# Strassen's scheme in the up projection of a gated MLP, with the down projection as a second stage, on one Trainium2 core

## The reference, cut to what matters

```python
D_MODEL, D_FF, DEPTH, CONV_W = 1024, 2816, 2, 3
def conv_gated_mlp(h, w_up, conv_w, conv_b, w_down):
    u = h @ w_up                              # (tokens, 2 * 2816)
    up = jnp.pad(u, ((0, 0), (1, 1), (0, 0)))
    c = conv_b
    for i in range(CONV_W):                   # width 3 along the tokens, each channel by itself
        c = c + up[:, i:i + s] * conv_w[i]
    gate, val = jnp.split(c, 2, axis=-1)
    return (jax.nn.gelu(gate, approximate=True) * val) @ w_down
...
x = x + rms_norm(conv_gated_mlp(rms_norm(x, norm_ffn_pre[l]), ...), norm_ffn_post[l])
```

## Time and profile before

| | |
|---|---|
| median of 3 runs | 3652.87 us (3652.32 to 3656.74) |
| the profiled execution | 3653.27 us |
| its span in the profile | 3651.5 us |
| PE busy | 3561.5 us (98%), 17785 matmuls |
| DVE, ACT, POOL busy | 50%, 42%, 32% |
| mean traffic of the DMA engines | 64 GB/s |
| MLP of the first layer | about 917 to 1870 us |
| MLP of the second layer | about 2721 us to the end |

### The profile page before, as it was taken

One profiled execution on the slowest core, in us unless ns is written; L12 is line 12 of the kernel. 1 busy time (PEld: TensorE's weight loads), 2 busy tenths in 40 slices (PEclk: granted clock), 3 DMA queues, 4 the chain that ended last, 5 costly groups with the idle time before them and its releaser, 6 DMA issues. The chain is left out here.

```text
span 3651.5 us, 49117 instructions
## 1 busy us (share of the span) xinstructions
PE 3561.5 (98%) x17785; PEld 2948.8 (81%) x17785; DVE 1837.5 (50%) x3004; ACT 1523.0 (42%) x2535; POOL 1153.3 (32%) x841
## 2 busy tenths in 40 slices
PE   8999999999999999999999999999999999999998
PEld 7788777778888888888767887777778888888886
DVE  4134879946333334343551358799353333433335
ACT  4344878955221222211342368788442122211213
POOL 1143554434322212211342435544342212211213
PEclk9999999999999999999999999999999999999999
DMA  5442221023111111111324423111221111111113
GB/s 176 124 114 69 77 69 34 23 81 104 47 35 40 38 37 34 40 40 34 115 68 136 123 55 86 49 41 39 95 79 41 41 34 40 40 34 34 40 41 115
DMA packets 235044, 234.10 MB, mean 64 GB/s; under 512 B 42188, under 2 KB 196126, under 8 KB 234847
## 3 DMA queue, kind: packets, MB, share of 16 engines
q1 hardware_dynamic: 234887, 232.09, 21.6%
HBM read 173.86 MB, written 51.48 MB: 62 GB/s over the span
## 5 line engine op out<-in xcount | busy, mean ns | idle before, releaser
L241 PE MATMUL ps<-hh,wh 128*128 128x512 f32 (+1 forms) x2544 | 917.7, 361 | 17.6 <-PEq L235 13.7
L242 PE MATMUL ps<-hl,wh 128*128 128x512 f32 (+1 forms) x2544 | 905.2, 356 | 0.0
L243 PE MATMUL ps<-hh,wl 128*128 128x512 f32 (+1 forms) x2544 | 904.2, 355 | 0.0
L2580 POOL TENSOR_TENSOR wl<-raw,wh 128x1024 fp32r<-128x1024 f32 x126 | 301.8, 2402 | 1270.2 <-ACT wh L2413 1270.2
L2641 DVE SCALAR_TENSOR_TENSOR cb<-ps,params,cb 128x1023 f32<-128x1023 f32 (+1 forms) x172 | 143.9, 878 | 872.7 <-ACT cb L2422 872.7
L241 PEld LDWEIGHTS ps<-hh,wh 128*128 128x128 f32 x2544 | 483.8, 190 | 92.2 <-issue 20.2
L242 PEld LDWEIGHTS ps<-hl,wh 128*128 128x128 f32 x2544 | 483.8, 190 | 72.9 <-issue 5.7
L243 PEld LDWEIGHTS ps<-hh,wl 128*128 128x128 f32 x2544 | 483.3, 190 | 68.4
L1661 DVE TENSOR_TENSOR pl<-ps,ph 128x512 fp32r<-128x512 f32 (+1 forms) x576 | 376.1, 653 | 67.0 <-ACT ps L1492 66.2
L1384 PE MATMUL ps<-q,k 97*128 97x512 f32 (+4 forms) x1296 | 387.1, 390 | 17.4 <-DVE pl L1661 7.5
L2422 ACT ACTIVATE cb<-ps,params 128x1280 f32<-128x1280 f32 x86 | 122.1, 1420 | 648.0 <-PE ps L243 638.2
(11 more groups left out here) (286 smaller groups left out, 5802.7 us busy)
## 6 DMA issues: line engine op xcount, KB each, us to landing
raw<-in_w_up SPq DMA_DIRECT2D x88, 512.0 KB, 3.8
raw<-in_w_down SPq DMA_DIRECT2D x44, 512.0 KB, 3.5
heads<-stage SPq DMA_DIRECT2D x28, 640.0 KB, 3.6
rq<-heads SPq DMA_DIRECT2D x56, 320.0 KB, 4.0
raw<-in_w_in SPq DMA_DIRECT2D x32, 512.0 KB, 4.2
rk<-heads SPq DMA_DIRECT2D x32, 320.0 KB, 4.6
raw<-in_w_out SPq DMA_DIRECT2D x16, 512.0 KB, 4.2
residual<-my SPq DMA_DIRECT2D x32, 256.0 KB, 2.0
```

What stands on the lines that cost most here:

```text
L241: pe.matmul(out, wh, xh, start=(k == 0), stop=False)
L242: pe.matmul(out, wh, xl, start=False, stop=False)
L243: last = pe.matmul(out, wl, xh, start=False, stop=(k == len(pairs) - 1))
L2580: pool.tensor_tensor(c.wl[slot][:], c.raw[parity][:], c.wh[slot][:].bitcast(F32), ALU.subtract).then_inc(w_lo, units)
```

## The change

In the pairs 2 to 21 of each layer (20 of 22) the prompt's part of the up projection is made with seven block products in place of eight. For one pair the weights are four blocks of 512 x 128: A11 and A12 (gate; first and last 512 features), A21 and A22 (value); the activations are four blocks of 512 features x 512 tokens, B11, B12, B21, B22. A block product is 4 chunks x 3 products, 12 matmuls of 512 columns. The form is Winograd's:

- of the weights, for each pair: S1 = A21 + A22, S2 = S1 - A11, S3 = A11 - A21, S4 = A12 - S2 (`weight_sum`, on POOL)
- of the activations, once in a layer: T1 = B12 - B11, T2 = B22 - T1, T3 = B22 - B12, T4 = T2 - B21. POOL rebuilds B11 and B21 from high and low parts (`rebuild`, 8 additions), DVE makes the forms (`t_forms`, 16 operations), ACT their high parts (`t_high`, 16), DVE (`t_lows`, 8) and POOL (`t_low`, 8) their low parts; all are 512 wide
- products: A11 B11, S2 T2, S3 T3, S1 T1, A12 B21, S4 B22, A22 T4; the sample (256 tokens) keeps its four plain block products (`sample`)
- of the results, for each pair, 512 wide: `keep_p1` and `keep_c11` on ACT, `second_sum`, `third_sum`, `corner22`, `corner12` and `corner21` on DVE, each with one input in PSUM. They leave the pair's prompt part in `u_gate` and `u_val`, which are in SBUF.

Each of the eight operands of a pair is split into a high part (ACT, `operand`) and a low part (POOL, `low_operand`), 512 wide, and has one slot, which is free for the next pair when its product is done. ACT's centre is now two instructions for each of gate and value: 1024 wide from `u_gate` or `u_val`, and 256 wide from PSUM; DVE's taps of the prompt, 1023 wide, have both inputs in SBUF, those of the sample still read PSUM. The product of gate and value is one operation 1280 wide; it is stored to memory (`store_act`, 640 KB for each pair). Pairs 0 and 1 are done as before (`plain`).

When all pairs are done, the down projection is a second stage of 11 steps, `down(it)` with `it` = 0 to 9 and the tail as the last: SP loads two weight tiles and 1280 KB of activations (`load_act`), ACT splits high parts (`down_weight`, `down_act`), POOL and DVE the low parts. Its matmuls are those of before; the first step copies into `y` in place of adding, so `y` needs no clearing. All loops are written out.

```diff
-                with pe.Fori(2, FF_PAIRS) as i:
-                    n = first(i)
-                    up(n, 1, 4 * i, 0)
-                    down(n + 1, (2, 0), i)
-                    up(n + 3, 1, 4 * i + 1, 1, downs=i)
-                    up(n + 4, 2, 4 * i + 2, 0)
-                    up(n + 5, 0, 4 * i + 3, 1)
+                plain(2, c.first_hi, c.first_lo, 0)
+                pe.wait_ge(second_lo, 1)
+                pe.wait_ge(val_shifted, 2)
+                plain(3, c.second_hi, c.second_lo, 1)
+                for j in range(FAST, FF):
+                    fast_pair(j)
+                for it in range(FF_PAIRS - 1):
+                    down(it)
                 tail()
...
+                def fast_pair(j):
+                    n = j - FAST
+                    pe.wait_ge(op_lo, op(j, A11))
+                    if n:
+                        pe.wait_ge(c11, n)
...
+                    fast_product(A11, 0, *block_of(0, 0)).then_inc(p1_done, 1)
+                    if n:
+                        pe.wait_ge(gate_shifted, 2 * (j - 1))
+                    sample(A11, GATE_BANK, 0, True, False)
+                    pe.wait_ge(op_lo, op(j, S2))
+                    if n:
+                        pe.wait_ge(u2_done, n)
+                    else:
+                        pe.wait_ge(t_lo_dve, 8)
+                    fast_product(S2, 1, *mixed(2)).then_inc(op_used, 1)
+                    pe.wait_ge(op_lo, op(j, S3))
...
+                    fast_product(S3, 2, *mixed(3)).then_inc(op_used, 1)
+                    pe.wait_ge(op_lo, op(j, S1))
...
+                    fast_product(S1, 3, *mixed(1)).then_inc(op_used, 1)
+                    pe.wait_ge(op_lo, op(j, A12))
+                    pe.wait_ge(p1_kept, n + 1)
+                    fast_product(A12, 0, *block_of(4, 0), onto=True).then_inc(p2_done, 1)
+                    sample(A12, GATE_BANK, 4, False, True)
+                    pe.wait_ge(op_lo, op(j, S4))
+                    pe.wait_ge(c22, n + 1)
+                    fast_product(S4, 3, *block_of(4, 512), onto=True).then_inc(op_used, 1)
+                    pe.wait_ge(op_lo, op(j, A22))
...
+                    fast_product(A22, 4, *mixed(4)).then_inc(p4_done, 1)
...
+                    sample(A22, VAL_BANK, 4, True, False)
+                    pe.wait_ge(op_lo, op(j, A21))
+                    sample(A21, VAL_BANK, 0, False, True)
```

ACT's part of it (the list for one pair, and the waits of three of its steps):

```diff
+                def operand(j, q):
...
+                    else:
+                        act.wait_ge(weight_sums, 4 * (j - FAST) + SUMS[q])
+                    if j > FAST:
+                        act.wait_ge(op_used, op(j - 1, q))
...
+                def gate_centre(j):
+                    act.wait_ge(act_stored, 16 * j)
...
+                    act.wait_ge(c11, j - FAST + 1)
+                    act.wait_ge(c12, j - FAST + 1)
...
+                for j in range(FAST, FF):
+                    if j > FAST:
+                        keep_p1(j)
+                    if j < LAST:
+                        for q in (A11, S2, S3, S1):
+                            operand(j + 1, q)
...
+                    keep_c11(j)
+                    if j < LAST:
+                        for q in (A12, S4):
+                            operand(j + 1, q)
...
+                    gate_centre(j)
+                    if j < LAST:
+                        operand(j + 1, A22)
+                    gelu(j)
+                    val_centre(j, 0)
+                    val_centre(j, 1)
+                    if j < LAST:
+                        operand(j + 1, A21)
```

and DVE's list for one pair:

```diff
+                for j in range(FAST, FF):
+                    second_sum(j)
+                    third_sum(j)
+                    corner22(j)
+                    corner12(j)
...
+                    gate_taps(j)
+                    corner21(j)
+                    val_taps(j, 0)
+                    val_taps(j, 1)
+                    gate(j)
```

More of the change, by code:

```diff
@@ L2112, in gated_mlp, with op, down_bank, last_use @@
     LOWS_ON_POOL = 6
-    def first(i):
-        return 4 + 6 * (i - 1)
+    FAST = 2
+    LAST = FF - 1
+    A11, S2, S3, S1, A12, S4, A22, A21 = range(8)
+    SUMS = {S1: 1, S2: 2, S3: 3, S4: 4}
+    GATE_BANK, VAL_BANK = 6, 7
+    def op(j, q):
+        return 8 * (j - FAST) + q + 1
+    ALL_OPS = op(LAST, 7)
+    def down_bank(it, u):
+        return ([0, 1, 2, 5, 6, 3, 4, 7] if it == 0 else [6, 7, 0, 1, 2, 3, 4, 5])[u % 8]
+    def last_use(it, u):
+        b = down_bank(it, u)
+        return max(n for n in range(24 * it + u) if down_bank(*divmod(n, 24)) == b)
     with ExitStack() as ex:
@@ L2178, in wait_copied, with up_raw, op_source, down_weights @@
             engine.wait_ge(copied_act, n + 1 - on_dve)
+        def up_raw(j):
+            return c.up_raw[1 - j % 2]
+        def op_source(j, q):
+            gate, val = up_raw(j)
+            return {A11: gate[:, 0:4, :], A12: gate[:, 4:8, :], A21: val[:, 0:4, :], A22: val[:, 4:8, :],
+                    S1: c.sum_a[:], S2: c.sum_b[:], S3: gate[:, 0:4, :], S4: gate[:, 4:8, :]}[q]
+        def down_weights(it):
+            return c.dw[0 if it == 0 else 1 if it % 2 else 2]
+        def down_raw(n):
+            return (c.up_raw[1][n] if n < 2 else c.raw[n % 2])[:]
@@ L2227, in _, with plain @@
             def _(pe):
-                def up(n, slot, m, half, downs=None, wait=True):
-                    if wait:
-                        pe.wait_ge(w_lo, n - 1)
-                    if downs is not None:
-                        pe.wait_ge(down_added, downs * 24 - 2)
-                    if wait:
-                        pe.wait_ge(shifted, m - 1)
-                    project(pe, c, slot, half).then_inc(w_used, 1)
-                def down(n, slots, it, wait=True):
-                    pe.wait_ge(w_lo, n)
-                    pe.wait_ge(act_lo, it)
-                    pe.wait_ge(act_lo1, it * 3)
+                def plain(unit, hi, lo, half):
+                    for b, (t0, w) in enumerate(BLOCKS):
+                        last = product(pe, bank(c, 3 * half + b, w), [(hi[:, k, :], lo[:, k, :], c.hh[:, k, t0:t0 + w], c.hl[:, k, t0:t0 + w])
+                                                                      for k in range(KC)])
+                    last.then_inc(plain_done, 1)
@@ new lines, in fast_product @@
+                def fast_product(q, b, xh, xl, onto=False):
+                    for k in range(4):
+                        out, wh, wl = bank(c, b), c.op_hi[q][:, k, :], c.op_lo[q][:, k, :]
+                        pe.matmul(out, wh, xh(k), start=(k == 0 and not onto), stop=False, skip_group_check=onto)
+                        pe.matmul(out, wh, xl(k), start=False, stop=False, skip_group_check=onto)
+                        last = pe.matmul(out, wl, xh(k), start=False, stop=(k == 3), skip_group_check=onto)
+                    return last
@@ new lines, in block_of, with mixed, sample @@
+                def block_of(k0, t0):
+                    return lambda k: c.hh[:, k0 + k, t0:t0 + 512], lambda k: c.hl[:, k0 + k, t0:t0 + 512]
+                def mixed(i):
+                    return lambda k: c.t_hi[i][:, k, :], lambda k: c.t_lo[i][:, k, :]
+                def sample(q, b, k0, first, last):
+                    out = bank(c, b, 256)
+                    for k in range(4):
+                        wh, wl, xh, xl = c.op_hi[q][:, k, :], c.op_lo[q][:, k, :], c.hh[:, k0 + k, 1024:T], c.hl[:, k0 + k, 1024:T]
+                        pe.matmul(out, wh, xh, start=(first and k == 0), stop=False)
+                        pe.matmul(out, wh, xl, start=False, stop=False)
+                        mm = pe.matmul(out, wl, xh, start=False, stop=(last and k == 3))
+                    mm.then_inc(op_used, 1)
@@ new lines, in _ @@
+                plain_val_centre(0)
+                act.activation(c.second_hi[:], c.raw[1][:], ACT.Copy).then_inc(second_hi, 1)
+                gelu(0)
+                t_high(0)
+                t_high(1)
+                gate_centre(1)
+                operand(FAST, A11)
+                t_high(2)
+                operand(FAST, S2)
+                gelu(1)
+                t_high(3)
+                plain_val_centre(1)
+                for q in (S3, S1):
+                    operand(FAST, q)
@@ new lines, in plain_taps, with gate_taps @@
+                def plain_taps(j, val):
+                    pieces = [(t0, s, unit_psum(c, val, t0, t0 + s)) for t0, s in SEGS]
+                    if val:
+                        taps(j, 1, pieces, (val_centred, 2 * (j + 1)), val_shifted, 2)
+                    else:
+                        taps(j, 0, pieces, (gate_centred, 2 * j), gate_shifted, 2)
+                def gate_taps(j):
+                    taps(j, 0, [(0, 1024, c.u_gate[:]), (1024, 256, bank(c, GATE_BANK, 256))], (gate_centred, 2 * j), gate_shifted, 2)
```

626 lines of the change are left out of this document (439 added, 187 removed).

## The result

The changed kernel takes **3571.7 us** (median of 4 runs, 3570.27 to 3576.23) against 3654.0 in the same session: a ratio of 0.9776, 95% interval 0.9759 to 0.9793, some 82 us less. The forecast was 3593, with 3550 to 3636 as its range. The profiled execution is the slowest of the four, 3576.23 us with a span of 3574.3: 77.0 less than the profiled one of before.

A forecast was written before the change was run, and what follows sets the result against it. PE, busy 98% of the span, was taken to bound the kernel. Terms -108.5 + 35 + 16 + 3 + 1.4 - 6.7 = -59.8 took 3653.3 to 3593 us; range 3550 to 3636, the forecast case's own 3570 to 3615.

The forecast's parts named there:

- 480 matmuls: Up projection: 84 wide matmuls a pair instead of 96, over 20 pairs in each of two layers: -108.5 us.
- ring: Steady pairs: the lists of POOL, ACT and DVE form a 25.2 us ring, 0.45 over PE's pace: +16 us.
- waits of the start: Start of each layer's stage: PE waits at the first fast pair and the next pair's sample, 17.5 us a layer: +35 us.
- cold clock: Start of the stage: waits let the granted clock fall, about 2 us each restart, part inside the next wait: +3 us.
- handover: Down projection's first step: its copies stand on DVE behind the last pair's product, so PE waits: +1.4 us.
- entry of the tail: Tail of the down projection: begins without its former wait for the last unit's taps and splits: -6.7 us.
- five possible meetings: In the ring, two taps and the product delay POOL, POOL delays two gate taps: 0 to 5.8 us, 2.9 taken.
- its sign: Waits of 8 us or more at first fast pair's S2 or S3, 5 to 7 at next pair's first sample product.
- the sign of the ring: An idle of a few tenths of a us at the same place in every pair, pairs 25.0 to 25.5 us apart.
- its 16 operations: At the start, POOL must still do 16 operations (20 us) for the gate's centre of the first fast pair.
- full gain: Rival: DVE's taps and POOL do not delay each other; ring of 22.3 stays hidden, start costs 14: 3552 us, chance 0.2.
- Slower: Rival: ring at its full price of 28.1 us, +122 us, with a start of 22 a layer: 3711 us, chance 0.09.

The follow-up runs named there:

- the eighth product: Last product of each pair (A22) done twice, against the changed kernel, so 96 wide matmuls a pair again: 3671.3 us, ratio 1.0054 to the kernel before.
- The run that reads PSUM: Changed kernel with DVE's forms and low parts of the activations taking their second input from an idle PSUM bank (results not the MLP's): 3550.4 us, ratio 0.9719.
- the run with the centre first: Changed kernel with ACT's gate centre of each pair ahead of the high part of the next pair's S4: 3562.1 us, ratio 0.9757.

## Why the prediction was right, and where it was off

| Term | forecast, us | measured, us | from |
|---|---|---|---|
| 480 matmuls | -108.5 | -108.8 | 40 pairs x 2.72 (27.58 against 24.86) |
| ring | +16 | 0 | no wait between 1100 and 1400 us |
| waits of the start | +35 | +23.8 | waits view, both layers |
| cold clock | +3 | +11.1 | 34.9 less 23.8; see the clock, below |
| handover | +1.4 | +3.3 | waits at L289, 1.6 and 1.7 |
| entry of the tail | -6.7 | -6.2 | source views |
| sum | -59.8 | -76.8 | profiled executions: -77.0 |

**The products** came out as costed. That a matmul taken away is worth its whole pace was shown by the eighth product.

**The ring** is the term that failed, and it is nearly the whole error. Its mechanism was right and its size off: 25.2 us in the forecast, 24.4 in the trace. Its bare part was 22.1 (22.3 forecast): 24.4 less the turns. The turns were the step mis-sized. I priced five possible meetings at half their worst, 2.9 us. There are two and a bit: POOL loses 0.98 at S1's sum, 1.14 at S2's and 0.13 at A21's low part (1.42 at 1298.83 us), 2.25 in all, and the gate's taps lose nothing. And PE's pair is 24.86, not 24.74. Together the excess of 0.45 became a slack of 0.48. A ring within 2% of PE's pace was too close to be told from rows of another stage: 0.9 us decided over 16 us. That the result lies in the forecast's own range (3570 to 3615) owes something to luck, since its central case, a ring over PE's pace, is not what happened. In this steady stretch meetings were not an average over random moments either: they recurred at the same place in each pair, so they were there or not.

**The start.** The places and the releasers were right: the S2 product for DVE's low parts, the next sample product for the gate's taps. The lateness was put at 11 and 6.5 us; the waits up to S2 were 6.8 and 8.2, those at the sample 4.5 and 4.3. So neither wait reached the size that the prediction gave as its sign (8 us or more, and 5 to 7), and the sign of the ring, pairs 25.0 to 25.5 us apart, was absent. The working added DVE's and POOL's times as if nothing overlapped (47.7 us); in the trace a good part of DVE's list falls where POOL waits for ACT, and then costs 0.69 an operation. The run that reads PSUM showed the turns as cause, the run with the centre first that some two thirds of the second wait are ACT's order, a link that the prediction counted in its start as in its ring: its 16 operations run to the S4 sum of pair 3.

**The clock.** I gave 3 us for restarts, part of each inside the next wait; by the table they are 11.1. The granted clock is 0.87 on average over the 45 us in which the waits lie, so what runs between two waits is slow too. But the table splits by the waits view, and so it undersells the forecast. By the distances between PE's starts, some 2.5 us of slow matmuls in each layer lie between the wait at S2 and the one at pair 3's sample, and what ended that second wait did not hang on PE. POOL worked back to back from 974.64 us up to S4's sum, and ACT waited for that sum (the second layer shows the same):

```profile
988.77 1.29 POOL L2883 TENSOR_TENSOR raw<-raw,sum_b 128x512 f32<-128x512 f32 x1
...
990.09 0.63 ACT L2645 ACTIVATE hh<-raw 128x512 fp32r<-128x512 f32 x1 [4.23 <-POOL raw L2883]
990.63 1.23 ACT L2595 ACTIVATE c_gate<-u_gate,params 128x1024 f32<-128x1024 f32 x1
```

At full clock PE would have come earlier and waited these 2.5 us longer. Counted so, and by the distances between starts, PE was 7.1 and 8.5 us late at S2 and about 7 at the sample: some 30 us in all against 35, and the clock took some 5 against 3. These two sizes are an estimate from the distances. The second lateness was then forecast well and the first too high. The two errors of the start offset each other either way: 38 forecast, 34.9 measured. That part of the agreement is luck.

**The handover** was undersized, 1.4 for 3.3. DVE's timeline:

```profile
1476.63 2.60 DVE L2999 TENSOR_TENSOR c_gate<-c_gate,c_val 128x1280 f32<-128x1280 f32 x1
1479.16 3.13 DVE L3090 COPY y<-ps 128x512 f32<-128x512 f32 x6
```

The product of the last pair takes 2.60 us, not 1.49: it meets POOL's low part of the first down weights, 1024 wide. These are the same turns as in the ring, which I did not apply here.

**Transfers** were costed at nothing, and were nothing: the weights land in 5.0 us in the median where it was 3.8 in the earlier trace rows, and no wait of PE in the stretch ends on one.

The rivals: "full gain" (ring hidden, start 14, 3552) had the ring's effect right, though not its reason (turns are there), and the start too cheap by 21. "Slower" was refuted for this kernel, but its mechanism is real: two operations more on POOL make it.

## What to carry to other kernels

When PE's part of a loop is shortened, work out for every other engine not its busy share but the ring that its list closes with the others', and look for the one link that closes it: here one place in ACT's list was worth 109 us as soon as POOL had two operations more, with POOL idle a quarter of the time. A hidden ring a few tenths under the pace is a cliff; give it slack before it is needed, by moving what nobody waits for behind what everybody waits for. In stretches where DVE and POOL both have work, cost their sum, unless the DVE operation has an input in PSUM, and find the stretches in which one of them is idle anyway. Then cost what a wait of PE does to the clock of the work behind it.

## What was not expected of the hardware

- DVE and POOL at full rate do not share evenly: a 512-wide DVE operation with two SBUF inputs goes from 0.68 to 1.78 us, one of POOL beside it from 1.29 to about 1.75, but in the steady pairs the product (1493) loses nothing while POOL's S2 sum beside it takes 2433. In the rows of one pair above, the one that starts second pays each time, DVE at 1299.13, POOL at 1300.21 and 1302.56; no run was made to turn the order round.
- An operation added to POOL in one place lengthened DVE's in another by 0.5 us, since it shifted the two lists against each other; a cost of 1.38 us gave 1.35 in spite of 0.48 of slack.
- Removing 13.5 us of waits at the start gave 21 us; the other 7 were matmuls that start closer together, at a granted clock of 0.96 in place of 0.87.
